# Short convolution and forgetting attention on one core: the order of work within a head pair laid out anew on four engines

## Time and profile before

| | us |
|---|---|
| median of 3 runs | 1236.54 |
| lowest and highest | 1235.18, 1238.55 |
| the profiled execution, its own time | 1232.4 |
| its span, first to last instruction | 1230.6 |
| TensorE busy in it | 1127.2 |

### The profile page before, as it was taken

One profiled execution on the slowest core, in us unless ns is written; L12 is line 12 of the kernel. 1 busy time (PEld: TensorE's weight loads), 2 busy tenths in 40 slices (PEclk: granted clock), 3 DMA queues, 4 the chain that ended last, 5 costly groups with the idle time before them and its releaser, 6 DMA issues.

```text
span 1230.6 us, 15338 instructions
## 1 busy us (share of the span) xinstructions
PE 1127.2 (92%) x5434; PEld 923.2 (75%) x5434; DVE 772.3 (63%) x1160; ACT 600.6 (49%) x1022; POOL 577.4 (47%) x404
## 2 busy tenths in 40 slices
PE   7999999999999999999888988889888898878898
PEld 5788888888888777877667777677776777757787
DVE  6997766786652274105676776767667686686551
ACT  5543232323433254215757657567665676675320
POOL 4255655555546453122554546454464544645320
PEclk9999999999999999999989999999998999999999
DMA  5201111011353132535110011110111011101332
GB/s 206 69 1 69 69 69 69 1 69 69 106 162 111 52 87 52 145 121 154 35 36 23 31 52 35 36 35 21 50 35 52 18 31 40 35 14 39 120 132 91
DMA packets 47565, 81.30 MB, mean 66 GB/s; under 512 B 4609, under 2 KB 29313, under 8 KB 47490
## 3 DMA queue, kind: packets, MB, share of 16 engines
q1 hardware_dynamic: 30706, 71.93, 18.1%
q10 hardware_dynamic: 16784, 8.39, 2.3%
HBM read 63.27 MB, written 17.04 MB: 65 GB/s over the span
## 4 chain that ended last, share of the span: by engine, by line
PE 61%; DVE 16%; issue 9%; ACT 8%; POOL 4%; DMA 1%; ACTq 0%; DVEq 0%; SPq 0%
PE ps L683 24%; PE ps L659 15%; PE ps L911 6%; PE ps L766 6%; PE ps L818 4%; DVE neg_max L1818 3%; PE ps L838 2%; DVE pt_lo L1832 2%; POOL k L2117 2%; DVE y L1848 2%; PE ps L857 1%; POOL p_small L2106 1%; ACT p_big L1293 1%; ACT pt_hi L1306 1%; ACT w_hi L1049 1%
## 5 line engine op out<-in xcount | busy, mean ns | idle before, releaser
L659 PE MATMUL ps<-h_hi,w_hi 128*128 128x512 f32 x504 | 215.7, 428 | 5.7 <-DVE y L1966 3.5
L2024 POOL TENSOR_TENSOR a_lo<-raw,a_hi 128x512 fp32r<-128x512 f32 x94 | 137.3, 1472 | 145.8 <-ACT a_hi L1077 145.7
L659 PE MATMUL ps<-h_hi,w_lo 128*128 128x512 f32 x504 | 204.4, 406 | 0.0
L659 PE MATMUL ps<-h_lo,w_hi 128*128 128x512 f32 x504 | 203.7, 404 | 0.0
L683 PE MATMUL ps<-b_hi,a_hi 128*128 128x512 f32 x456 | 179.0, 393 | 3.2 <-DVE b_lo L1539 3.1
L683 PE MATMUL ps<-b_lo,a_hi 128*128 128x512 f32 x456 | 177.5, 389 | 0.0
L683 PE MATMUL ps<-b_hi,a_lo 128*128 128x512 f32 x456 | 177.4, 389 | 0.0
L818 PE MATMUL ps<-k,q 128*128 128x512 f32 (+5 forms) x384 | 96.4, 361 | 46.2 <-DVE q L1853 21.7
L2106 POOL TENSOR_TENSOR p_big<-p_big,rdenom 128x896 f32<-128x896 f32 (+1 forms) x64 | 78.5, 1227 | 117.6 <-DVE rdenom L1826 117.6
L1832 DVE TENSOR_TENSOR pt_lo<-ps,pt_hi 128x512 fp32r<-128x512 f32 (+1 forms) x160 | 97.0, 631 | 55.8 <-ACT pt_hi L1306 55.4
L1077 ACT ACTIVATE a_hi<-raw 128x512 fp32r<-128x512 f32 x94 | 57.9, 628 | 119.4 <-DMA raw<-in_w_cin 43.1
(11 more groups left out here) (194 smaller groups left out, 2340.2 us busy)
## 6 DMA issues: line engine op xcount, KB each, us to landing
raw<-in_w_cin SPq DMA_DIRECT2D x28, 512.0 KB, 4.5
w_raw<-in_w_ain SPq DMA_DIRECT2D x24, 512.0 KB, 3.5
xy<-in_x SPq DMA_DIRECT2D x16, 512.0 KB, 4.9
v_st<-v_dram SPq DMA_DIRECT2D x16, 512.0 KB, 3.7
v_dram<-v_out ACTq DMA_DIRECT2D x10, 512.0 KB, 5.7
raw<-in_w_cout SPq DMA_DIRECT2D x8, 512.0 KB, 4.3
x_dram<-xy SPq DMA_DIRECT2D x8, 512.0 KB, 4.2
vw_raw<-in_w_ain SPq DMA_DIRECT2D x16, 256.0 KB, 3.3
```

Source lines behind the costliest of these rows:

```text
L659: last = mm(ps[:, bank, :], st[slot][:, k, :], mov(k)[:, halves(h)], start=(at == 0 and (when or k == 0) and st is w_hi and mov is mov_hi) ...
L2024: TT(a_lo[:, i % RING, :, :], entry_source(i), a_hi[:, i % RING, :, :].bitcast(F32), ALU.subtract).then_inc(s_alo, 1)
```

## The change

The tensors and the products stay the same; what changes is which engine does y's gate and where each step of work stands in each engine's queue.

1. `PLAN` is new: the same 48 pieces, distributed otherwise over the places of the eight steps (steps 0 to 7 hold 8, 7, 4, 7, 7, 8, 4, 3 pieces for 9, 6, 5, 4, 8, 6, 5, 5). Pair 0 uses it too.
2. In the middle pairs y's gate (`out_gate`) moves from VectorE to GpSimd. In the last pair it stays on VectorE.
3. In the middle pairs the calls on ScalarE, VectorE and GpSimd stand in another order. On ScalarE the split of weights moves behind the exp of step 3 and to the end of step 5, the silu to the head of step 2, q's high part behind the second exp. On VectorE the lower part of q moves to the head of step 7, z's evacuation to its end. On GpSimd the lower part of k moves to the end of step 2 and to the head of step 7, and starts after the first of ScalarE's two copies (`s_khi` counts both).
4. The forget gate's sums (parts 1 to 3) move from pair 0 to the values' phase; SP stores them after six slices, and loads the rows after the last slice.
5. In the values, `slices_used` counts the second group's slices anew (a slot is free one slice earlier there).
6. In the last pair, the first two output units go by k in turn from the first block on; y2's low part of block 1 goes to GpSimd; the first row maximum stands ahead of two of y2's low parts; k's last high and low parts are made a step earlier. All of y2's high parts follow the last exp.

```diff
-PLAN = ((3, 1, 1, 1, 2, 1, 0, 0), (2, 0, 1, 1, 0, 1, 1, 0), (2, 0, 1, 0, 1, 1, 0, 0), (2, 0, 1, 0, 1, 0, 0, 0),
-        (3, 0, 1, 1, 2, 1, 0, 0), (2, 0, 1, 1, 0, 1, 1, 0), (2, 0, 1, 0, 1, 1, 0, 0), (2, 0, 1, 1, 1, 0, 0, 0))
+PLAN = ((3, 0, 1, 3, 0, 0, 1, 0), (2, 0, 0, 1, 1, 1, 2, 0), (0, 0, 0, 1, 0, 3, 0, 0), (2, 0, 4, 0, 1, 0, 0, 0),
+        (1, 2, 0, 0, 2, 2, 0, 0), (3, 1, 0, 1, 0, 2, 1, 0), (1, 1, 0, 0, 0, 1, 1, 0), (2, 1, 0, 0, 0, 0, 0, 0))
-BY_VECTOR, BY_GPSIMD = [0, 1, 2, 3, 6], [4, 5]
+BY_VECTOR, BY_GPSIMD = [0, 2, 3, 6], [1, 4, 5]
-AHEAD_PIECES = ([(u, k) for u in range(2) for k in range(KH)]
-                + [(u, k) for k in range(KH, KT - 1) for u in range(2)]
+AHEAD_PIECES = ([(u, k) for k in range(KT - 1) for u in range(2)]
                 + [(u, k) for u in range(2, 2 * AHEAD) for k in range(KT - 1)])
+        def slices_used(engine, n):
+            if n == KT:
+                engine.wait_ge(s_vd, KT)
+            elif n > 0:
+                engine.wait_ge(s_vus, n - n // KT)
 SP, pair 0:
-                        load_slice(2)
-                        store_c()
+                        for j in range(2, V_SLICES):
+                            load_slice(j)
+                            if j == 5:
+                                store_c()
                         sp.wait_ge(s_cst, 64)
                         sp.wait_ge(s_clear, 8)
                         c_rows(0, it)
-                        for j in range(3, V_SLICES):
-                            load_slice(j)
 ScalarE:
-                A(k1[own, side, :], kn[own, :], ACT.Copy)
+                A(k1[own, side, :], kn[own, :], ACT.Copy).then_inc(s_khi, 1)
 ScalarE, values:
+                        if j == V_RING:
+                            forget(1)
+                            forget(2)
 ScalarE, iteration (steady = proj and att):
+                    if steady and i == 0: split(it, 1)
+                    if steady and i == 2: z_silu(it - 1)
                     if att: softmax_exp(it, i, 0)
+                    if steady and i == 3: split(it, 2)
                     for c in range(min(2, chunks)): pt_split(own, at, c)
+                    if steady and i == 2: guess(it, 0)
+                    if steady and i == 5: guess(it, 2)
+                    if steady and i == 6: guess(it, 3)
+                    if steady and i == 7: stack_k_hi(it, 0)
+                    if steady and i == 1: square(it, 0)
                     if chunks > 2: pt_split(own, at, 2)
+                    if steady and i == 4: guess(it, 1)
+                    if steady and i == 0: stack_q_hi(it - 1, 1)
                     if att: softmax_exp(it, i, 1)
+                    if steady and i == 2: stack_k_hi(it - 1, 1)
                     if chunks > 3: pt_split(own, at, 3)
+                    if steady and i == 3: square(it, 1)
+                    if steady and i == 6: stack_q_hi(it, 0)
                     if chunks and STEPS[at][1] % 2 == 0: out_copy(own, at)
+                    if steady and i == 5: split(it, 3)
+                    if steady and i == 4: square(it, 2)
+                    if steady and i == 5: square(it, 3)
 VectorE, iteration:
+                    if steady and i == 7: stack_q_lo(it, 0)
                     if att: invert(it, i, 0)
                     for c in range(min(2, chunks)): pt_low(own, at, c)
-                    if proj and i == 7: z_evac(it, 0)
                     if att: row_max(it, i, 1)
                     for c in range(2, chunks): pt_low(own, at, c)
-                    if att and i and STEPS[i - 1][1] in (1, 3) and (i >= 2 or (before and proj)):
-                        out_gate(*((it, i - 2) if i >= 2 else (it - 1, 7)))
                     if att: invert(it, i, 1)
                     if proj and i in UNIT_NORMED: local = refine(...)
-                    if proj and i == (6 if last else 7): stack_q_lo(it, 0)
+                    if steady and i == 7: z_evac(it, 0)
 GpSimd, iteration:
+                    if steady and i == 1: weights_low(it, 1)
+                    if steady and i == 7: stack_k_lo(it, 0)
+                    if steady and i == 1: square_lo(it, 0)
+                    if steady and i == 5: square_lo(it, 2); out_gate(it, 3)
+                    if steady and i == 7: out_gate(it, 5)
                     if att: normalise(it, i, 0)
+                    if steady and i == 6: weights_low(it, 3)
                     if att: normalise(it, i, 1)
+                    if steady and i == 2: stack_k_lo(it - 1, 1)
+                    if steady and i == 3: square_lo(it, 1)
+                    if steady and i == 5: square_lo(it, 3)
+                    if steady and i == 3: weights_low(it, 2)
+                    if steady and i == 0 and it > 1: out_gate(it - 1, 7)
+                    if steady and i == 2: out_gate(it, 1)
...
```

More of the change, by code:

```diff
@@ L1374, in values, with split @@
                     v_store(KT * (g + 1) - 1)
+            def split(it, t):
+                n = N_AIN + 3 * it + t
+                split_w(n, n % 2, n // 2)
             def iteration(it, proj, att, before, last=False):
+                steady = proj and att
                 for i in range(8):
@@ L1388, in iteration @@
                         softmax_exp(it, i, 0)
+                    if steady and i == 3:
+                        split(it, 2)
                     for c in range(min(2, chunks)):
@@ L1918, in iteration @@
                         add_ahead(i - 1)
+                    if steady and i == 0 and it > 1:
+                        z_evac(it - 1, 1)
+                    if steady and i == 7:
+                        stack_q_lo(it, 0)
+                    if not att and i == 7:
+                        stack_q_lo(it, 0)
                     if att:
@@ L1922, in iteration @@
                         pt_low(own, at, c)
-                    if proj and i == 7:
+                    if not att and i == 7:
                         z_evac(it, 0)
@@ L1928, in iteration @@
                         y2_low(6)
-                    if att and i == 0:
+                    if not proj and i == 0:
                         stack_q_lo(it - 1, 1)
@@ L1970, in _ @@
             z_evac(0, 1)
+            for part in range(1, 4):
+                forget(part)
             for n in range(2 * KT):
```

171 lines of the change are left out of this document (120 added, 51 removed), and 7 rows, old and new, of the table PLAN.

## The result

The changed kernel takes 1153.32 us (median of four runs, 1151.65 to 1155.78) beside 1235.86 for the kernel before, measured with it: ratio 0.9334, 95% interval 0.9306 to 0.9361. The profiled execution took 1155.78 (span 1154.0).

A forecast was written before the change was run, and what follows sets the result against it. TensorE's own waits were taken as the bound. Gains of 37 us (seven middle pairs), 5.3 (pair 0), 1.5 (values) and 8.1 (last pair) made 52: 1232.4 to 1180.5, plus 4.1 gives 1185 us, range 1166 to 1210.

The forecast's parts named there:

- the work of a pair: Middle pair: TensorE's work and handovers without waits and slow clock, about 62.7 us of 75.0.
- The clock: Middle pair: half of the 1.7 us lost at the low clock is saved, 0.9 (bounds 0 and 1.7).
- Rival 1: Middle pairs: waits only move and VectorE and GpSimd collide; gain 2.3 us a pair, 1205 us in all; chance 22%.
- full price of 5.2 a pair: Middle pairs: each of four gates on GpSimd holds VectorE for its 1.3 us; total gain shrinks from 52 to 16.
- the sum of waits in a middle pair: TensorE's waits per middle pair, transposes' included, fall from 10.6 to 6.2 us, 4.4 less.
- three signs of being wrong: Transposes waiting for GpSimd's normalising, VectorE's first refinement steps well past 0.7 us, or a larger share of slow clock.
- Start of a pair: Step 7 to next scores: waits of 0.35 + 3.6 us become 3.5 (2.3 for a p part, 1.2 for the exp).
- Change of side: Middle pair: k's lower part moves from step 3 to the end of step 2; its 2.3 us wait goes to 0.
- The other waits: Middle pair: remaining waits for p parts, 3.45 us, become 2.6 including new ones for exp, mean square and handovers.
- the transposes' 0.1: Middle pair: the transposes' 0.9 us wait for GpSimd's normalising goes, but for 0.1.
- Rival 3: Middle pairs: full clock throughout and small waits vanish; gain 7.5 us a pair, 1170 us in all; chance 13%.
- the added 4.1: Total: 4.1 us added to 1180.5 because the median shown before lay that far above the profiled execution.

The follow-up runs named there:

- e4: The kernel before with only y's four gates of a middle pair moved to GpSimd, order and plan as before: 1240.21 us, ratio 1.0085.
- e9: The changed kernel with y's evacuation in step 7 back between the p parts and the second row maximum: 1162.93 us, ratio 0.9416.
- e15: The changed kernel with VectorE's former order in the middle pairs (gates on VectorE, q's lower part and y's evacuation at their old places): 1174.01 us, ratio 0.9513.
- e7: The changed kernel with k's second lower part back between step 3's normalisings on GpSimd: 1160.06 us, ratio 0.9418.
- e16: The changed kernel with k's second lower part back in step 3 and the weights' lower part at that step's head, on GpSimd: 1187.91 us, ratio 0.9628.
- e17: The changed kernel with GpSimd's and ScalarE's former orders in the middle pairs and the gates on VectorE: 1190.85 us, ratio 0.9664.
- e13: The changed kernel with ScalarE's former order in the middle pairs: 1187.16 us, ratio 0.9638.
- e8: The changed kernel with the forget gate's sums and slices' loads back in pair 0, and the last pair's k parts a step later: 1165.03 us, ratio 0.9451.
- e2: The changed kernel with the former plan of pieces in the middle pairs, pair 0 keeping the new one: 1142.08 us, ratio 0.9285.
- e5: The changed kernel with two pieces of step 5 moved to step 7 in the middle pairs: 1147.47 us, ratio 0.9322.
- e11: The changed kernel with the former plan of pieces in the middle pairs, measured again beside the changed kernel: 1142.21 us, ratio 0.9261.
- e18: The changed kernel with the former plan of pieces in the middle pairs and the gates back on VectorE: 1146.23 us, ratio 0.9292.

## Why the prediction missed

**Right.** The bound (TensorE's own waits, at most some 12 us a pair), the work of a pair (62.7), and each named cause: no wait for q or k; a wait of about 2 for a p part in step 7 (1.82); gates of 1.28 us on GpSimd for 1.3; the forget sum behind the first values' products (473.34, they begin at 468.43); no wait for the add. The clock gave 1.1 us a pair for 0.9 (the seven pairs' lengths times 1 - PEclk to two places: 18.3 before, 10.9 after). Rival 1's collisions do not hold VectorE: in the middle pairs all 28 first refinement steps in its trace take 0.67 and all 14 lower parts of q 1.22, and no gate on GpSimd has one of these beside it. Each refinement step starts 0.16 us ahead of a GpSimd normalising, and it is the normalising that is longer (128x512: 1.41 beside a step, 1.04 elsewhere). The Trainium skill (SBUF — State Buffer, section Who interferes with whom) lets the one that comes later wait; the trace agrees. So the full price of 5.2 a pair, which the prediction weighed, was never due. The trace of the kernel before has the same 28 steps at 0.66 to 0.68, each as far ahead of its normalising: the prediction's argument against rival 1 is right here, and could have been read from that trace. Only e4, with another order, has one of its collisions (q's lower part, 2.07).

**The step that failed is the sum of waits in a middle pair: "10.6 become 3.5 + 0 + 2.6 + 0.1 = 6.2".** It became 3.15. That is 3.05 a pair, 21.4 us in seven, nearly all of the 22 us by which the pairs beat their 37. None of the prediction's three signs of being wrong came; all three stood for a smaller gain. Three terms:

1. *Start of a pair, "0.35 + 3.6 becomes 3.5".* It became 2.4. The exp's 1.2 was read from the earlier trace rows, where 1.3 us lie between p parts and exp; 0.68 of them are y's evacuation, which the change moves behind, and the prediction did not cost that move. e9 puts it back and finds the 1.2. (The working's "some 2.1" is also 0.3 more than the 1.3 and 0.47 that it names; between the exp's end and the scores lie 0.24 in e9 and 0.26 in the changed kernel.) The p part's wait was 0.5 too high. VectorE's order with the gates is worth 2.7 a pair (e15); the forecast had 0.45 of waits and 0.9 of clock.
2. *Change of side, "2.3 goes to 0".* Right in size; but k's earlier step alone is worth only 0.5 of it (e7), and the weights' lower part that no longer stands ahead of k the rest (e16).
3. *The other waits, "together 2.6", and the transposes' 0.1.* They are 0.7: 0.43 behind the silu for 0.9, 0.29 of step 1 for 0.45, and nothing that the trace lists for the mean square, step 6 and the handovers. e17 gives the two orders that feed these places, and k, 4.6 a pair together; the forecast had 3.95 for them (2.3, 0.85 and 0.8).

e15 and e17 make 7.3 of the 8.5 a pair (both have the gates in them); what the remaining 1.2 belongs to is not settled, as effects do not add here (the plan, which costs 1.9 to 2.2 a pair, is in none of these). Of the small waits in term 3, step 6's is shown to hang on q's two copies in ScalarE's queue: 1.88 with them ahead (e13), none without, for the 0.3 that the forecast left. For the others there is no run of their own; that they were put too high because every edit was costed on the old queue, with its own lateness left in, is argued and not shown.

**The rest.** Rival 3 named the right direction (7.5 a pair, 1170), and even it was too small. Pair 0 gained 6.4 for 5.3, of which the forget gate's place carries 2.3 (e8), not nearly all. The last pair's 9.8 for 8.1 rests on k, as forecast. In the total, the 24.7 us between 1180.5 and the profiled 1155.78 are 22.3 in the pairs, 1.7, 1.1 and 0.3 at the ends, less the start's 0.6; the added 4.1 made the forecast worse, since the profile after was the slowest run of its four.

## What to carry to other kernels

When a queue's order is changed, write out the new order of each engine and time the late operation in it; a gap read from the old trace holds whatever stood in it, and may be moved too. Orders of engines that hand parts to each other are one thing: put back alone, ScalarE's or GpSimd's order cost as much as both or more, and the gate moved alone made the kernel 0.9% longer. After a reordering, look again at the work that covers the waits: two pieces moved into the step with the last two waits were worth more than the gate's engine.

## What the runs showed of the hardware

The clock follows the waits, not evenly. All seven pairs of e2, e5 and e11 run at 1.00 throughout; after the first, none of them has a wait over 1.22 us. Behind a wait of 1.82 and one of 0.61, the first 3.5 us of a pair of the changed kernel are now at the high level and now mostly at the 1.2 GHz one:
```profile
693.88:697.38 3.50, 3.50 (x17) 2.94 (x18) 2.61 (x5) 1.75 (x3) 1.98 (x3) 1.00 0.01 2
827.22:830.72 3.50, 3.50 (x10) 2.89 (x11) 2.60 (x5) 1.53 (x2) 1.98 (x3) 0.60 0.00 1
```
That is 1.5 us a pair, and it adds to the price of a wait (e9: 3.4 us more of waits in the seven pairs, 5 to 7 more of time). What decides between the two isn't shown. It is not the longest wait alone: the first pair of e11 has one of 2.02 and runs at 1.00, the first pair of e18 has one of 2.07 and a stretch at the low clock (PEclk 0.98 over the pair).

Either engine's instruction can be the one that is stretched when VectorE and GpSimd meet on tensors in SBUF, and in these traces it is the one that begins second. Of the kernel before, y's gate on VectorE (0.68 elsewhere) and k's lower part on GpSimd (2.35 elsewhere), at the change of side and then at the pair's end:
```profile
825.07 0.68 DVE L1848 TENSOR_TENSOR y<-osum,y 64x512 f32<-64x512 f32 x1
825.20 2.75 POOL L2117 TENSOR_TENSOR k<-kn,k 64x1024 fp32r<-64x1024 f32 x1
...
861.51 2.35 POOL L2117 TENSOR_TENSOR k<-kn,k 64x1024 fp32r<-64x1024 f32 x1 [1.13 <-ACT k L1336]
```
The gate that began 0.13 ahead kept its time and k's part was stretched; the gate of 862.25 began 0.74 behind and took 2.16. The running sum of 16x1024 on VectorE fits: it took 4.24, begun 0.31 behind a GpSimd subtraction of 2.40, and 3.19 in the changed kernel, begun 0.88 behind one of 1.93. GpSimd's lower part of k, which began during that 3.19, took 4.37 for its usual 2.4.
